# Last projection tile ahead of the key tiles, accumulator slots by name, and four recurrent halves of the output projection moved into the end of the attention

## The reference

```
h = rms_norm(x, norm1_g) * (1 + scale1) + shift1
z = h @ w_in
x_lru, g_lru, q_lat, kv_lat, k_rope = split(z)      # 512, 512, 256, 128, 32 columns
lru_out = rg_lru(causal_dwconv(x_lru)) * gelu(g_lru)
q  = rms_norm(q_lat) @ w_uq          # 8 heads of 64 + 32 (rotated)
kv = kv_lat @ w_ukv                  # 8 heads of 64 keys + 64 values, keys normalised
attn = softmax(mask(q_nope @ k_nope + q_rope @ k_rope) * scale) @ v
mixed = concat(rms_norm(lru_out), rms_norm(attn)) @ w_o
x = x + gate1 * mixed
h2 = rms_norm(x, norm2_g) * (1 + scale2) + shift2
x = x + gate2 * ((gelu(gt) * val) @ w_down)         # val, gt = split(causal_dwconv(h2 @ w_up))
```

## Time and profile before

| what | value |
|---|---|
| median of the runs | 994.62 us (994.04 to 997.07) |
| the profiled execution | 996.8 us, its span 995.0 us |
| mean granted clock of TensorE | 0.984 of full speed |
| PE busy | 955.5 us (96% of the span) |
| DVE busy | 659.1 us (66%) |
| ACT busy | 528.2 us (53%) |
| POOL busy | 183.1 us (18%) |
| DMA | 100 GB/s over the span |

### The profile page before, as it was taken

One profiled execution on the slowest core, in us unless ns is written; L12 is line 12 of the kernel. 1 busy time (PEld: TensorE's weight loads), 2 busy tenths in 40 slices (PEclk: granted clock), 3 DMA queues, 4 the chain that ended last, 5 costly groups with the idle time before them and its releaser, 6 DMA issues.

```text
span 995.0 us, 20681 instructions
## 1 busy us (share of the span) xinstructions
PE 955.5 (96%) x8014; PEld 889.2 (89%) x8014; DVE 659.1 (66%) x1259; ACT 528.2 (53%) x1183; POOL 183.1 (18%) x186
## 2 busy tenths in 40 slices
PE   5799999999999999999998999999999999999997
PEld 3488876689999999999987989999999999999997
DVE  2694276568987988989774556777777777722221
ACT  2333843389889898898873333444444443321210
POOL 0022220233334333433210230100100100000000
PEclk9799999899999999999999989999999999999999
DMA  9967630600202202122101531333333332662202
GB/s 342 335 186 253 209 131 6 230 1 23 86 23 94 99 23 86 56 73 86 43 23 43 149 57 44 84 95 108 93 84 84 84 86 65 165 160 62 63 3 87
DMA packets 106291, 100.14 MB, mean 101 GB/s; under 512 B 7120, under 2 KB 94944, under 8 KB 104127
## 3 DMA queue, kind: packets, MB, share of 16 engines
q1 hardware_dynamic: 102422, 77.91, 26.9%
q0 software_dynamic: 3456, 20.97, 5.9%
q10 hardware_dynamic: 340, 0.27, 0.1%
HBM read 96.41 MB, written 2.94 MB: 100 GB/s over the span
## 4 chain that ended last, share of the span: by engine, by line
PE 87%; DVE 6%; ACT 3%; DMA 2%; issue 2%; SPq 0%; DVEq 0%; ACTq 0%
PE ps L874 50%; PE ps L1255 19%; PE ps L869 7%; PE ps L907 2%; PE ps L1162 2%; PE ps L1213 2%; DMA RW<-w_ada 2%; PE ps L1250 1%; PE ps L1188 1%; DVE RB L1933 1%; PE ps L880 1%; DVE normed_low L1834 1%; PE ps L1044 1%; DVE RB L1808 0%; ACT RB L1437 0%
## 5 line engine op out<-in xcount | busy, mean ns | idle before, releaser
L874 PE MATMUL ps<-normed_high,up_weights_high 128*128 128x260 f32 x704 | 142.1, 283 | 0.2
L874 PE MATMUL ps<-normed_high,up_weights_low 128*128 128x260 f32 x704 | 141.9, 283 | 0.0
L874 PE MATMUL ps<-normed_low,up_weights_high 128*128 128x260 f32 x704 | 141.6, 283 | 0.0
L1674 ACT ACTIVATE up_weights_high<-RW 128x1024 fp32r<-128x1024 f32 x44 | 46.6, 1061 | 136.1 <-PE ps L874 133.3
L832 POOL TENSOR_TENSOR latents_low<-RB,latents_high 128x512 fp32r<-128x512 f32 (+1 forms) x72 | 86.2, 1198 | 169.5 <-ACT latents_high L1569 169.5
L1255 PE MATMUL ps<-key_weights_high,latents_high 128*128 128x260 f32 x528 | 116.4, 302 | 0.7 <-ACT RB L1616 0.6
L874 PEld LDWEIGHTS ps<-normed_high,up_weights_high 128*128 128x128 f32 x704 | 108.6, 188 | 0.8 <-DVE normed_low L1834 0.6
L874 PEld LDWEIGHTS ps<-normed_high,up_weights_low 128*128 128x128 f32 x704 | 108.6, 188 | 0.0
L874 PEld LDWEIGHTS ps<-normed_low,up_weights_high 128*128 128x128 f32 x704 | 108.2, 188 | 0.0
L1255 PE MATMUL ps<-key_weights_low,latents_high 128*128 128x260 f32 x528 | 106.3, 283 | 0.0
L1255 PE MATMUL ps<-key_weights_high,latents_low 128*128 128x260 f32 x528 | 106.3, 283 | 0.0
(11 more groups left out here) (316 smaller groups left out, 2205.4 us busy)
## 6 DMA issues: line engine op xcount, KB each, us to landing
RW<-w_ada SPq DMA_DIRECT2D x24, 1024.0 KB, 7.4
RW<-w_up SPq DMA_DIRECT2D x44, 512.0 KB, 5.1
RW<-w_down SPq DMA_DIRECT2D x8, 1408.0 KB, 7.3
RW<-w_in SPq DMA_DIRECT2D x11, 512.0 KB, 6.9
RB<-w_o SPq DMA_DIRECT2D x8, 512.0 KB, 4.3
RB<-x_prompt SPq DMA_DIRECT2D x2, 1024.0 KB, 12.9
o_y_p<-RB SPq DMA_DIRECT2D x4, 512.0 KB
cst<-consts SPq DMA_DIRECT2D x1, 845.0 KB, 9.7
```

What stands on the lines that cost most here:

```text
L874: last = mm(ps[j % 4][rows[0]:rows[1], h, 0:H], lhsT, src[:, h * H:(h + 1) * H], start=start, stop=stop)
L1674: A(wuH[:, KT * g:KT * g + KT, :], wup[:, c, KT * g:KT * g + KT, :], ACT.Copy).then_inc(s_whi, 1)
```

## The change

**Input and prep.** Projection tile 11 (with modulation chunk 15) moves in front of key tiles 0 and 1 on PE. `PREP_ORDER` now names each job's slot, and its order is `c5`, `qst`, `l0` to `l3`, `kv2`, `kv3`, `qa`, `spread`, `l4` to `l6`, `nlru`. The dummies after the first query tile go from 6 to 3, and two lots of 3 (after key tile 1, among the stored rows) are left out. On DVE, scans 2 and 3 move behind the first two query tiles; the product of scan and GELU stands ahead of the sums of the key tiles; the copies of stored rows stand between the key tiles' steps; and the norm of the recurrent half stands behind the split of the first unit's queries. On ACT, the last gate tile and GELU come before the squares of key tiles 0 and 1. ACT no longer waits for the norm (`s_mix`) before the latents; POOL does, before its first split.

**Last key unit.** The high parts of the recurrent half (ACT, four copies) and their low parts (POOL, four subtractions) are made inside the last unit, as are those of `w_o` tiles 0 and 1, which get buffers of their own; the last head's turned probabilities go to a part of `sq` (`hpt_last`) so that `recurrent_high` can use the place of `hpt`.

**End.** PE runs the recurrent halves of output tiles 0 and 1 in front of the turn of the maxima in place of eight dummies; shorter lots of dummies (2, 4, 2) stand in the softmax. The latent mix and the value product share one slot, with semaphores `s_olr` and `s_ol` between them. The recurrent half of tile 2 stands before the sum of squares, that of tile 3 behind it. Then come steps 4 to 7 of tiles 0, 1 and 2 together, those of tile 3, and tiles 4 to 7 whole. SP's loads of `w_o` tiles 3 and 4 wait for POOL's split of tiles 0 and 1, the later ones for DVE's of tiles 2 on.

The diff, cut to its core:

```diff
-               "q2", "q3", "kv0", "kv1", "w11"])
-PREP_ORDER = ["c5", "qst", "kv2", "kv3"] + [f"l{n}" for n in range(7)] + ["qa", "spread", "nlru"]
+               "q2", "q3", "w11", "kv0", "kv1"])
+PREP_ORDER = [("c5", 1), ("qst", 3), ("l0", 1), ("l1", 3), ("l2", 1), ("l3", 3), ("kv2", 2), ("kv3", 0), ("qa", 1), ("spread", 3),
+              ("l4", 1), ("l5", 3), ("l6", 2), ("nlru", 0)]
...
-J_OL, J_VP, J_NMLA = job(0), job(2), job(3)
-J_WO = [job(1)] + [job(3 + m) for m in range(1, KT)]
-J_N2, J_FST = job(3 + KT), job(4 + KT)
-UP0 = 5 + KT
+J_NMLA, J_VP = job(2), job(3)
+J_WO = [job(n) for n in (0, 1, 7, 6, 4, 5, 11, 10)]
+J_N2, J_FST = job(KT), job(KT + 1)
...
+        hpt_last = sq[:, 0:4, 0:NP]
...
+        woH0, woH1, woL0 = [nc.alloc_sbuf_tensor_at(f"first_output_weights{n}", [P, KT, P], FR, offset=at) for n, at in enumerate(first_at)]
+        woL1 = nc.alloc_sbuf_tensor_at("first_output_weights3", [P, KT, P], FR, offset=sq_at + 4 * 3120)
+        wo_high = [woH0[:, :, :], woH1[:, :, :]] + [woH[:, m % 2, :, :] for m in range(2, KT)]
+        wo_low = [woL0[:, :, :], woL1[:, :, :]] + [woL[:, m % 2, :, :] for m in range(2, KT)]
...
             for m in range(KT):
                 if m == 2:
                     kfull(sp, key_job(NS - 1, "k", KTILES - 1))
-                if m >= 3:
-                    sp.wait_ge(s_wolo, m - 2)
+                if 3 <= m < 5:
+                    sp.wait_ge(s_wflo, m - 2)
+                if m >= 5:
+                    sp.wait_ge(s_wolo, m - 4)
                 sp.dma_start(woR[m % 3], wo[:, :, P * m:P * m + P]).then_inc(s_wo[m % 3], 16)
...
+            def recurrent_low(k):
+
+                if k == 0:
+                    pool.wait_ge(s_out, 16 * 10)
+                pool.wait_ge(s_rhi, k + 1)
+                nc.gpsimd.tensor_tensor(mixed_low[k], hT[:, k, :], mixed_high[k].bitcast(F32), ALU.subtract).then_inc(s_rlo, 1)
+
+            def first_low(m):
+
+                bfull(pool, "pv", NS - 1)
+                pool.wait_ge(s_wfhi, m + 1)
+                nc.gpsimd.tensor_tensor(wo_low[m], woR[m], wo_high[m].bitcast(F32), ALU.subtract).then_inc(s_wflo, 1)
+
+            pool.wait_ge(s_mix, LT)
...
+                    if u == NS - 1 and 2 <= g < 2 + LT:
+                        recurrent_low(g - 2)
+                    if u == NS - 1 and g >= NG - 2:
+                        first_low(g + 2 - NG)
...
             w_in(10)
             later_chunk(14)
...
+            later_chunk(15)
             pe.wait_ge(s_kvn, 1)
             keys_and_values(0)
             keys_and_values(1)
-            keep_busy(spare, 3)
-            w_in(11)
-            later_chunk(15)
             mod_columns(5)
...
+            pe.wait_ge(s_kr, 2)
+            stored_rows(0)
+            stored_rows(1)
+            stored_rows(2)
+            stored_rows(3)
+            keys_and_values(2)
+            keys_and_values(3)
...
+            stored_rows(4)
+            pe.wait_ge(s_lrud, 1)
+            stored_columns(0, TA, NP - 1, 9)
+            stored_columns(1, XX, NP, 11)
...
                 unit(u)
-            for i in range(3):
-                pe.wait_ge(key_free[i], KEY_JOBS // 3)
-            keep_busy(ps[0][:, 0, 0:2 * P], 8)
+            def out_products(m, k):
+
+                j = J_WO[m]
+                for n, (w, src) in enumerate(((wo_high[m], mixed_high), (wo_high[m], mixed_low), (wo_low[m], mixed_high))):
+                    last = both(j, w[:, k, :], src[k], k == 0 and n == 0, k == KT - 1 and n == 2)
+                if k == KT - 1:
+                    last.then_inc(psum_full[j % 4], 1)
+
+            def out_weights(m):
+
+                if m < 2:
+                    pe.wait_ge(s_wflo, m + 1)
+                else:
+                    pe.wait_ge(s_wolo, m - 1)
+
+            def recurrent_half(m):
+
+                claim(pe, J_WO[m])
+                out_weights(m)
+                for k in range(LT):
+                    pe.wait_ge(s_rlo, k + 1)
+                    out_products(m, k)
+
+            for m in range(2):
+                pe.wait_ge(key_free[m], KEY_JOBS // 3)
+                recurrent_half(m)
+            pe.wait_ge(key_free[2], KEY_JOBS // 3)
             turn_max(NS)
+            keep_busy(ps[2][:, 0, 0:2 * P], 2)
             spread_max(NS)
-            keep_busy(ps[0][:, 0, 0:2 * P], 3)
+            keep_busy(ps[2][:, 0, 0:2 * P], 4)
             pv(NS)
+            keep_busy(ps[2][:, 0, 0:2 * P], 2)
 
...
             j = J_VP
             claim(pe, j)
-            pe.wait_ge(psum_free[J_OL % 4], free_value(J_OL))
+            for n in range(NS):
+                last = mm(flat(j)[:, HEADS * n:HEADS * n + HEADS], OLR[:, n, :], C("pick", HEADS), start=True, stop=True)
+            last.then_inc(s_olr, 1)
+            pe.wait_ge(s_ol, 1)
...
             last.then_inc(psum_full[j % 4], 1)
-            out_projection(0, (2, 3))
+            recurrent_half(2)
             norm_sum(J_NMLA, LT, KT + 8)
-
-            out_projection(1, range(LT))
-            out_projection(0, range(LT, KT))
-            out_projection(1, range(LT, KT))
-            for m in range(2, KT):
-                out_projection(m, range(KT))
+            recurrent_half(3)
+            for k in range(LT, KT):
+                pe.wait_ge(s_mlo, k - LT + 1)
+                for m in range(3):
+                    out_products(m, k)
+            for k in range(LT, KT):
+                out_products(3, k)
+            for m in range(4, KT):
+                claim(pe, J_WO[m])
+                out_weights(m)
+                for k in range(KT):
+                    out_products(m, k)
...
             nc.scalar.preload_act_table_set("natural_log_exp_and_others")
+            key_squares(0)
+            key_squares(1)
+            prep_rstd(5, HEADS)
+            act.wait_ge(s_lrud, 2)
+            lru_squares(0)
+            prep_rstd(6, HEADS)
+            lru_squares(2)
             key_squares(2)
             key_squares(3)
...
+                        if u == NS - 1 and (g, n) in RECURRENT_AT:
+                            recurrent_high(RECURRENT_AT.index((g, n)))
+                        if u == NS - 1 and g in (6, 7) and n == 1:
+                            first_high(g - 6)
+
+            def recurrent_high(k):
+
+                act.wait_ge(s_mix, LT)
+                A(mixed_high[k], hT[:, k, :], ACT.Copy).then_inc(s_rhi, 1)
+
+            def first_high(m):
+
+                bfull(act, "pv", NS - 1)
+                act.wait_ge(s_wo[m], 16)
+                A(wo_high[m], woR[m], ACT.Copy).then_inc(s_wfhi, 1)
...
+            out_high(2)
+            out_high(3)
...
             for a in range(2):
                 prep_sums(1 + a, query_sq, HEADS)
                 prep_query_tile(a)
+            scan(2)
+            scan(3)
...
+            dve.wait_ge(s_g, 1)
+            V.tensor_tensor(GG[:, :, :], TA[:, :, :], GG[:, :, :], MUL).then_inc(s_lrud, 1)
             mod_columns(5)
...
+            def lru_normed():
+                for k in range(LT):
+                    V.scalar_tensor_tensor(hT[:, k, :], GG[:, k, :], pr("lru_out_norm_g", k), rs[:, :], MUL, MUL).then_inc(s_mix, 1)
...
+            dve.wait_ge(s_rs, 5)
+            lru_normed()
...
+                dve.wait_ge(s_wohi, m - 1)
+                V.tensor_tensor(wo_low[m], woR[m % 3], wo_high[m].bitcast(F32), SUB).then_inc(s_wolo, 1)
+
+
+            out_low(2)
             finish(NS)
-            full(dve, J_OL)
+            dve.wait_ge(s_olr, 1)
...
+
+            out_low(3)
             dve.wait_ge(s_rs, 6)
```

More of the change, by code:

```diff
@@ L180, in number_jobs @@
         used[slot] += 1
-    for n, name in enumerate(PREP_ORDER):
-        jobs[name] = n % 4 + 4 * used[n % 4]
-        used[n % 4] += 1
+    for name, slot in PREP_ORDER:
+        jobs[name] = slot + 4 * used[slot]
+        used[slot] += 1
     return jobs, used
@@ L2032, in _ @@
             prep_keys(2)
[L2034 to L2044 removed]
+            prep_keys(3)
             full(dve, J_QA)
```

146 lines of the change are left out of this document (58 added, 88 removed).

## The result

The changed kernel took 985.13 us (median of 4 runs, 983.53 to 986.60), the kernel before in the same comparison 995.85 (4 runs): a ratio of 0.989, interval 0.9875 to 0.9905, so 9.5 to 12.4 us faster. The forecast was 981.4 with a range of 979.0 to 987.1. The direction and the range held; the gain came out at 10.7 us instead of 13.2.

What follows compares the result with a forecast made beforehand. Bounds: first key tile's start, when the last head's mixing reaches TensorE, and the output projection left. Gains of 5.2 (front) and 8.75 (end) less 0.7 (last key unit) made 13.2, so 994.62 became 981.4 us; range 979.0 to 987.1.

Steps and rivals of the forecast that it cites:

- The two stretches named at the start: TensorE between query tiles and first key product (141 to 201 us), and behind the last key tile (513 to 543 us).
- the walked order: Front: new order stepped through by old durations; query tile 1 at 142.4, tile 11 at 157.4, key tile 2's slot at 173.8.
- Rivals 2, 4 and 5: Key tiles' start set elsewhere, 986.6, 5%; second weight split late, 997.4, 4%; output weights landing late, 994.3, 5%.
- A: Way to the first key product: reordered input and prep bring it earlier by 5.2 us.
- tiles 2 and 3 ... end at 177.3: Front: after the slot frees at 173.8, four products of key tiles 2 and 3, 0.86 apart, end at 177.3.
- 4.5 to 5.9: Bounds in us for the front's gain: lower if the clock falls under key tiles 2 and 3, upper if not.
- B: Behind the last key tile: recurrent halves moved forward and shorter waits let the output projection end 8.75 us earlier.
- the lower of the bounds given (6.7): End of the kernel: gain of 6.7 us if half clock lasts through half 2 and part of the sum of squares.
- with dummies in its waits: Last softmax, from the turn of the maxima to the mixing, keeps its 3.1 us; dummy products fill TensorE's waits.
- C: Last key unit pays for added copies and splits, as POOL delays VectorE's scalings: 0.7 us lost, bounds 0 and 1.5.
- Rival 3: Last key unit: POOL's new work holds VectorE all along, costing some 6 us; 986.7 us, 6%.
- Rival 1: Front and end: the clock takes back more, gains falling to 3 and 5.2 us; 987.1 us, 18%.

Runs made afterwards that it cites:

- front alone: Kernel before with only the changes to input and prep, last key unit and end as before: 992.11 us, ratio 0.9959.
- end alone: Kernel before with only the changes to the last key unit and the end, input and prep as before: 990.66 us, ratio 0.9934.

## Why the prediction was right, and where its sizes were off

- **The direction and the places were right.** The two stretches named at the start are where the time went, and the parts are separate: front alone and end alone add up. Query tile 1, tile 11, the key squares and the slot of key tile 2 came within 0.3 us of the walked order, the two halves took 5.80 (forecast 5.8), the products after the first attention tile 34.7 (34.6), and no weights were late. Rivals 2, 4 and 5 did not come.
- **A was mis-sized by the clock.** The step that failed is "tiles 2 and 3 ... end at 177.3". It took both tiles at full speed, with a remark that 1.4 of 2 us would reach the sum if the clock fell. It fell in all eight profiles whose front has no added dummies, two of them with an order taken back (the first pair at 2.08 us in each). Key tiles 2 and 3 took 2.2 us more than the 3.4 assumed, the sum started at 185.28 for 183.0, and only the sum itself gave some back (5.14 instead of 6.02), so that the first key product came at 196.37 for 195.15. Against the two profiles of the old front (63.73 and 62.19, mean 63.0) the new one takes 58.7 to 59.9 (five profiles, mean 59.2): 3.8, where 5.2 was forecast. The bounds "4.5 to 5.9" rested on one profile of before, and the clock of that profile was itself part of the sum: its folded key queries and sum of squares were slow, and in the other one they took 1.3 us less. That the 4.9 of the first pair lies inside the bounds is luck of that profile.
- **B was right in its steps and took its cover for granted.** In the profile it gained 8.3 (8.75 forecast; the latent mix took 1.85, not 1.46, at the full clock). But five of the eight profiles with this end as it is have 62.0 us instead of 60.5, the half of output tile 2 being at half clock: a gain of 6.8, the lower of the bounds given (6.7). The mean of the eight is 7.4. By the forecast's own sign ("It would be wrong if the clock is at 0.50 where products of the output projection run") these five speak against it; only the changed kernel's own profile and two others don't. The forecast called the softmax "with dummies in its waits" and gave them no price; without them 3.6 to 5.2 us go.
- **C was the mechanism named, at the upper end.** "The last head's probabilities are scaled beside such a split once, for up to 1.3": one scaling met a new split and was 0.83 longer, as said; a second was 0.54 longer beside a split of latents that was there before. The key units grew by 1.2 in the first pair and by 1.3 in the means (0.7 taken, bound 1.5). Rival 3, POOL holding DVE all along, is out: a reduction of DVE took 0.68 from 499.94 on while POOL subtracted from 499.55 to 500.86, as elsewhere. The Trainium skill (SBUF — State Buffer, "SBUF: two separate sides") in full says that the lock bears on instructions of DVE in a two-port mode or with two inputs from SBUF; the reductions, with one input, agree, and whether the scalings run in such a mode no run here shows.
- **The sum.** 3.8 + 7.4 - 1.3 - 0.2 for the rest = 9.7 with the means of the profiles; timed 10.7, interval 9.5 to 12.4. The forecast's 13.2 was too large by what the clock took in both places. Rival 1 (18%, 987.1) was the right mechanism in half its strength: A fell to 3.8, not 3, and B to 6.8 in five of eight, not 5.2. The range reached over it, and so it held.

What stays open: what decides, in one and the same code, whether the clock falls behind the latent mix (three of eight profiles not, five yes); how the front's gain divides, beyond the places of scans, tile 11 and ACT's wait; and 0.5 us of the last unit.

## What to carry to other kernels

Where a chain leaves TensorE waiting, price the clock along with the wait: here a wait of 1.7 us cost 2.2 more on the products behind it, and eight dummy products were worth 3.6 to 5.2 us in the profiles and some 3 in the timed runs. Fill such places with real work that is due anyway, as the recurrent halves were, and with dummies where there is none; then look at the granted clock, not at the idle time alone. And take a term from more than one profile before its bounds are drawn: the old front differed by 1.5 us between two profiles of the same code.

## What had not been expected of the hardware

- In the kernel without dummies the clock stayed at 0.50 from 520 to 532 us (0.72 from 518 to 520) with PE busy for 12.9 of the 14 us from 518 on.
- Three dummies in the 1.7 us wait kept the clock in two kernels and not in a third with the same code up to that place (pairs of products at 1.02 and at 1.9 us).
- The start of the program, up to the rotation product, took between 134.3 and 138.3 us in profiles whose code for PE is the same up to there: these 4 us are more than the spread of the changed kernel's timed runs (3.1).
